# Turned tiles taken out of the attention units, and the filler matmuls taken out of the chunk inverses, in a two-block decoder kernel

## The reference, cut to what matters

```python
def rwkv7_scan(r, w, k, v, a, b):
    # S_t = S diag(w_t) + (S a_t) b_t^T + v_t k_t^T ;  y_t = S_t r_t
    def step(S, inp):
        r_t, w_t, k_t, v_t, a_t, b_t = inp
        Sa = jnp.einsum('bhij,bhj->bhi', S, a_t)
        S = S * w_t[:, :, None, :] + Sa[..., None] * b_t[:, :, None, :] + v_t[..., None] * k_t[:, :, None, :]
        return S, jnp.einsum('bhij,bhj->bhi', S, r_t)
```

## Time and profile before

| | us |
|---|---|
| median of 3 runs | 3400.59 |
| the runs | 3396.19 to 3407.80 |
| the profiled execution | 3394.34 |
| its span | 3392.6 |
| PE busy | 3306.0 (97%) |
| DVE busy | 1931.4 (57%) |
| ACT busy | 1254.7 (37%) |

### The profile page before, as it was taken

How to read it: one execution, slowest core, us unless ns; L and a number is a source line. 1 busy time by engine, 2 the same in 40 slices (tenths; PEclk the granted TensorE clock), 3 DMA queues, 4 the chain that set the end, 5 groups by cost and what they waited for, 6 DMA issues and landing times.

```text
span 3392.6 us, 50022 instructions
## 1 busy us (share of the span) xinstructions
PE 3306.0 (97%) x18459; PEld 2704.5 (80%) x18459; DVE 1931.4 (57%) x3749; ACT 1254.7 (37%) x1622; POOL 132.2 (4%) x54
## 2 busy tenths in 40 slices
PE   8998999999899999999999999999999999999998
PEld 6665877878577788888878887888888888888886
DVE  5455456552565544452355999998885444444443
ACT  3333233322455433342343334444544333333332
POOL 0000000000000000000001545000000000000000
PEclk9987999999999999999999999999999999999999
DMA  4110012323222222222332444455556655555542
GB/s 145 56 38 1 4 51 81 99 93 100 86 65 67 80 76 79 80 74 93 100 106 79 148 141 143 156 180 182 185 177 220 228 198 192 198 194 196 198 142 81
DMA packets 145995, 408.03 MB, mean 120 GB/s; under 512 B 11225, under 2 KB 43993, under 8 KB 143585
## 3 DMA queue, kind: packets, MB, share of 16 engines
q1 hardware_dynamic: 73520, 265.85, 25.7%
q10 hardware_dynamic: 72368, 140.68, 11.5%
HBM read 337.28 MB, written 69.21 MB: 120 GB/s over the span
## 4 chain that ended last, share of the span: by engine, by line
PE 87%; DVE 10%; ACT 1%; issue 1%; DMA 1%; ACTq 0%; DVEq 0%; SPq 0%
PE bank L337 24%; PE bank L339 24%; PE bank L338 24%; PE bank L959 2%; PE bank L445 2%; PE bank L957 2%; PE bank L889 1%; ACT arena L1000 1%; PE bank L464 1%; DVE arena L2057 1%; PE bank L503 1%; DVE arena L2020 1%; DVE arena L2021 1%; DVE arena L2023 1%; PE bank L372 1%
## 5 line engine op out<-in xcount | busy, mean ns | idle before, releaser
L337 PE MATMUL bank<-xs,ring_hi 128*128 128x512 f32 x2488 | 990.9, 398 | 19.9 <-DVE xs L1564 9.7
L339 PE MATMUL bank<-xs,ring_lo 128*128 128x512 f32 x2488 | 971.8, 391 | 0.0
L338 PE MATMUL bank<-xs,ring_hi 128*128 128x512 f32 x2488 | 971.3, 390 | 0.0
L1000 ACT ACTIVATE arena<-bank 128x512 f32<-128x512 f32 (+4 forms) x584 | 392.1, 706 | 1013.1 <-PE bank L339 726.8
L1000 ACT ACTIVATE ring_hi<-ring 128x1024 fp32r<-128x1024 f32 x503 | 532.4, 1061 | 621.4 <-DMA ring<-weights 425.3
L1557 DVE TENSOR_TENSOR ring_lo<-ring,ring_hi 128x1024 fp32r<-128x1024 f32 x246 | 300.2, 1224 | 519.5 <-ACT ring_hi L1000 484.0
L337 PEld LDWEIGHTS bank<-xs,ring_hi 128*128 128x128 f32 x2488 | 468.8, 188 | 127.9 <-issue 14.4
L339 PEld LDWEIGHTS bank<-xs,ring_lo 128*128 128x128 f32 x2488 | 468.3, 188 | 100.9
L338 PEld LDWEIGHTS bank<-xs,ring_hi 128*128 128x128 f32 x2488 | 469.2, 189 | 97.1 <-issue 3.4
L2070 DVE TENSOR_TENSOR ring_lo<-ring,ring_hi 128x1024 fp32r<-128x1024 f32 x206 | 252.6, 1226 | 387.3 <-ACT ring_hi L1000 387.2
L337 PE MATMUL bank<-gw,ring_hi 128*128 128x512 f32 x1024 | 398.5, 389 | 0.7 <-ACT arena L1000 0.7
(11 more groups left out here) (285 smaller groups left out, 3408.4 us busy)
## 6 DMA issues: line engine op xcount, KB each, us to landing
ring<-weights SPq DMA_DIRECT2D x503, 512.0 KB, 3.6
hidden<-arena ACTq DMA_DIRECT2D x128, 256.0 KB, 4.1
gates<-arena ACTq DMA_DIRECT2D x16, 2048.0 KB, 6.6
arena<-hidden ACTq DMA_DIRECT2D x16, 2048.0 KB, 10.3
arena<-gates ACTq DMA_DIRECT2D x16, 2048.0 KB, 16.9
xres<-x_t ACTq DMA_DIRECT2D x4, 512.0 KB, 6.5
out_t<-arena SPq DMA_DIRECT2D x4, 512.0 KB, 3.0
arena<-ret_decay ACTq DMA_DIRECT2D x1, 1024.0 KB, 5.9
```

Of the source, the lines that this page charges most:

```text
L337: pe.matmul(out_, wh, x[0], start=start, stop=False, skip_group_check=True)
L338: pe.matmul(out_, wh, x[1], start=False, stop=False, skip_group_check=True)
L339: return pe.matmul(out_, wl, x[0], start=False, stop=stop, skip_group_check=True)
L1000: return act.activation(out_, in_, f, **kw)
```

## The change

Two edits. First, the six turns of TA and TB for the pairs 0 to 2 leave the units and join the late turns, which become sixteen; the waits on `tok_out` and the semaphores `tok_ready` and `tok_out` go with them. Counts of `rw_act` and `rw_pe` behind the late turns rise by six (30 becomes 36). Second, the two `keep_clock(7, 1)` in each level of the inverses go, twenty in all. The fillers in the units and in the scan over chunks stay. What the kernel computes stays the same.

```diff
@@ PE, rw_prepare
-                if u in (19, 20, 23, 24, 27, 28):
-                    i, g0 = (u - 19) % 4, (u - 19) // 4
-                    pe.wait_ge(rw_dve, 2 * g0 + 2)
-                    if 2 * g0 + i:
-                        pe.wait_ge(tok_out, 2 * g0 + i)
-                    for g in range(TT):
-                        tr = pe.transpose(bank[1][:, g * P:(g + 1) * P], tile((TA, TB)[i] + g0)[:, g * P:(g + 1) * P], cc("ident"))
-                    tr.then_inc(tok_ready, 1)
                 if u in (17, 21, 25, 29):
                     pe.wait_ge(rw_dve, 2 * m + 1)
-                    if m:
-                        pe.wait_ge(tok_out, 2 * m)
                     pe.matmul(bank[1][:, :], cc("bones"), tile(RKR), start=True, stop=True).then_inc(rw_pe, 1)
@@ PE, late turns
             pe.wait_ge(rw_dve, 8)
-            pe.wait_ge(tok_out, 2 * (NPAIR - 1))
-            late = [(TA, 3), (TB, 3)] + [(TK, m) for m in range(NPAIR)] + [(RV, m) for m in range(NPAIR)]
-            for j, (src, m) in enumerate(late):
+            for i, (src, _) in enumerate(((TA, MA), (TB, MB), (TK, MK), (RV, MV))):
+                for m in range(NPAIR):
+                    j = 4 * i + m
                     if j >= 2:
                         pe.wait_ge(rw_act, 20 + j - 1)
@@ PE, levels of the inverse
                         pe.wait_ge(rw_dve, 8 + RW_DVE * r + 2 * lev + s + 1)
-                        if s == 0:
-                            keep_clock(7, 1)
                         mm = chunks(bank[b0], tile(hs[2 + a]), tile(hs[a]))
...
                         a, b = (0, 1) if lev % 2 == 0 else (1, 0)
-                        if s == 0:
-                            keep_clock(7, 1)
-                        pe.wait_ge(rw_act, 30 + RW_ACT * r + 2 * lev + s + 1)
+                        pe.wait_ge(rw_act, 36 + RW_ACT * r + 2 * lev + s + 1)
                         chunks(bank[b0 + 2], tile(hs[b]), tile(hs[4 + a])).then_inc(rw_pe, 1)
@@ ACT, rw_prepare
-                if u in (20, 21, 24, 25, 28, 29):
-                    i, g0 = (u - 20) % 4, (u - 20) // 4
-                    act.wait_ge(tok_ready, 2 * g0 + i + 1)
-                    A(tile((MA, MB)[i] + g0), bank[1][:, :], ACT.Copy).then_inc(tok_out, 1)
@@ ACT, late turns
-            late = [(MA, 3), (MB, 3)] + [(MK, m) for m in range(NPAIR)] + [(MV, m) for m in range(NPAIR)]
-            for j, (dst, m) in enumerate(late):
-                act.wait_ge(rw_pe, 20 + j + 1)
-                A(tile(dst + m), bank[j % 2][:, :], ACT.Copy).then_inc(rw_act, 1)
+            for i, dst in enumerate((MA, MB, MK, MV)):
+                for m in range(NPAIR):
+                    act.wait_ge(rw_pe, 20 + 4 * i + m + 1)
+                    A(tile(dst + m), bank[(4 * i + m) % 2][:, :], ACT.Copy).then_inc(rw_act, 1)
```

More of the change, by code:

```diff
@@ L221, in build @@
         shifted = sem("shifted")
-        tok_ready, tok_out = sem("rwkv_by_token_psum"), sem("rwkv_by_token")
         ffn_pair, ffn_silu, root_arg = sem("ffn_pair"), sem("ffn_gate_activated"), sem("root_argument")
@@ L572, in _ @@
                     if r == 0:
-                        pe.wait_ge(rw_act, 30)
+                        pe.wait_ge(rw_act, 36)
                     else:
-                        pe.wait_ge(rw_act, 30 + RW_ACT - 1 + s)
+                        pe.wait_ge(rw_act, 36 + RW_ACT - 1 + s)
                         pe.wait_ge(rw_dve, 8 + RW_DVE)
@@ L633, in _ @@
                     hs, b0 = HS[s], 3 * s
-                    pe.wait_ge(rw_act, 30 + RW_ACT * r + 10 + 3 * s + 1)
+                    pe.wait_ge(rw_act, 36 + RW_ACT * r + 10 + 3 * s + 1)
                     chunks(bank[b0 + 2], tile(hs[5]), tile(hs[7])).then_inc(rw_pe, 1)
-            base_pe, base_act, base_dve = 30 + RW_PE * 2, 30 + RW_ACT * 2, 8 + RW_DVE * 2
+            base_pe, base_act, base_dve = 36 + RW_PE * 2, 36 + RW_ACT * 2, 8 + RW_DVE * 2
             shv = arena[:, SH:SH + 4, :].rearrange("p a b -> p (a b)").rearrange("p (c n) -> p c n", c=NCH)
@@ L1140, in _ @@
             pair_copy(NPAIR - 1)
-            late = [(MA, 3), (MB, 3)] + [(MK, m) for m in range(NPAIR)] + [(MV, m) for m in range(NPAIR)]
-            for j, (dst, m) in enumerate(late):
-                act.wait_ge(rw_pe, 20 + j + 1)
-                A(tile(dst + m), bank[j % 2][:, :], ACT.Copy).then_inc(rw_act, 1)
+            for i, dst in enumerate((MA, MB, MK, MV)):
+                for m in range(NPAIR):
+                    act.wait_ge(rw_pe, 20 + 4 * i + m + 1)
+                    A(tile(dst + m), bank[(4 * i + m) % 2][:, :], ACT.Copy).then_inc(rw_act, 1)
             for r in range(2):
-                pb = 30 + RW_PE * r
+                pb = 36 + RW_PE * r
                 for lev in range(5):
@@ L1165, in _ @@
                 A(XS[k][0], tile(OF + k), ACT.Copy).then_inc(hi_ready, 1)
-            bp = 30 + RW_PE * 2 + 22
-            ba = 30 + RW_ACT * 2
+            bp = 36 + RW_PE * 2 + 22
+            ba = 36 + RW_ACT * 2
             for m in range(NPAIR):
@@ L1703, in _ @@
             st(TTN(dv(2)[:, :, 0:NCH - 1], dv(1)[:, :, 0:NCH - 1], dv(0)[:, :, 1:NCH], ALU.mult))
-            ve.wait_ge(rw_act, 30)
+            ve.wait_ge(rw_act, 36)
             def mask8(name, half):
@@ L1715, in _ @@
                     if r:
-                        ve.wait_ge(rw_act, 30 + RW_ACT - 1 + s)
+                        ve.wait_ge(rw_act, 36 + RW_ACT - 1 + s)
                     for e in range(2):
@@ L1738, in _ @@
                         TTN(tile(hs[4 + b]), bank[b0 + 2][:, :], tile(hs[4 + a]), ALU.add).then_inc(rw_dve, 1)
-            bp, bd = 30 + RW_PE * 2, 8 + RW_DVE * 2
+            bp, bd = 36 + RW_PE * 2, 8 + RW_DVE * 2
             shv = arena[:, SH:SH + 4, :].rearrange("p a b -> p (a b)").rearrange("p (c n) -> p c n", c=NCH)
@@ L1746, in _ @@
                 if c == 0:
-                    ve.wait_ge(rw_act, 30 + RW_ACT * 2)
+                    ve.wait_ge(rw_act, 36 + RW_ACT * 2)
                     CP(tile(UU + g)[trow, :], tile(U0 + g)[trow, :]).then_inc(rw_dve, 1)
@@ L1773, in _ @@
                 st.go(TSM(tile(RG + m), tile(RG + m), pp("ln_w", m), None, ALU.mult))
-            ba = 30 + RW_ACT * 2 + 4
+            ba = 36 + RW_ACT * 2 + 4
             for m in range(NPAIR):
```

## The result

The changed kernel takes 3362.68 us in the median of four runs (3355.97 to 3366.32), the kernel before 3398.39 us beside it (3393.74 to 3407.80). The profiled executions took 3394.34 us (before) and 3359.28 us (changed).

What follows compares the result with a forecast made beforehand. The prediction took PE's chain and its granted clock to bound the kernel. Its terms were 3394.3 - 11.0 + 4.0 - 7.7 - 3 = 3376.6 us; with 6.2 added the forecast was 3383 us, range 3367 to 3397.

Steps and rivals of the forecast that it cites:

- What bounds the kernel: Whole kernel: PE, busy in 97% of the span, holds the path; its granted clock is lower in slices three and four.
- The turned tiles: Attention units: six transpose groups (4.4 us) and PE's six waits for ACT (6.6 us) go, -11.0 us at unchanged clock.
- The late turns: Behind the last unit: six more turn-and-copy jobs of 0.67 us each, hidden by nothing, +4.0 us.
- Rival 4: Late turns: the longer run of sixteen drops the clock, costing some 5 us more, 3388 us; chance 0.05.
- The fillers: Inverses: 18 of twenty filler matmuls save 0.43 us each, -7.7 us, between -6.7 and -8.6.
- The clock in the units: Attention units: effect of the edits on the granted clock, bounded by -14 and +14 us, taken as -3 us.
- rival 1: Attention units: the clock stays up in most of them, -14 us there, 3372 us in all; chance 0.18.
- The offset: Whole kernel: +6.2 us added because the profiled execution was that much faster than the median of three runs.
- the sum of 3376.6: Whole kernel: forecast in us against the profiled execution, all edit and clock terms included, before 6.2 us were added.
- Rival 3: Inverses: without fillers the clock falls to 0.50, +56 us in both rounds, 3438 us; chance 0.07.

Runs made afterwards that it cites:

- run 1: The kernel before with only the twenty filler matmuls of the inverses taken out, turned tiles still in the units: 3382.4 us, ratio 0.9968.
- run 3: The changed kernel with the six turns back in the units, through banks 1 and 0, copied early so PE doesn't wait: 3354.5 us, 0.9884 of the kernel before.
- run 4: The changed kernel with PE's waits for ACT's copies put back in units 20, 21, 24, 25, 28, 29, without turns: 3389.0 us, 0.9990 of before.
- run 9: The changed kernel with only the waits for ACT's copies in units 21, 25 and 29 put back, no turns: 3390.0 us, 0.9987 of before.
- run 8: The changed kernel with only the waits for ACT's copies in units 20, 24 and 28 put back, no turns: 3374.1 us, 0.9948 of before.
- run 7: The kernel of run 3 without the 22 filler matmuls in and around the scan over chunks: 3359.8 us, 0.9885 of the kernel before.
- run 10: The changed kernel with two fillers in a row at each place in the inverses where the kernel before had one: 3373.1 us, executed once.

## Why the prediction was wrong

- **What bounds the kernel** was right: PE's chain and its clock, in the third and fourth slice.
- **The turned tiles**: the waits went as said. L546's became a wait for DVE, 1.5 us in three, which the prediction had excluded on the ground that DVE was idle for half of the stretch. That idle time was at half clock; at full clock DVE is 93% busy.
- **The late turns**: +4.0 us forecast, 7.22 to 11.24 = +4.0 measured, at clock 1.00. Rival 4, and with it the Trainium skill's rule that transposes don't count as busy ("TensorE: Matmul & The Clock Gate", Part 4: PE-mode transpose), would have dropped the clock in this stretch. The row shows sixteen turns at 1.00; the measurement decides. (The trace books them as plain MATMUL; whether they run in the mode that the page speaks of, no row shows.)
- **The fillers**: forecast -7.7 us with a bound at -8.6, measured -9.8 (two rounds of -4.88; run 1: -10.1). The count of 18 and the cover by ACT and DVE were right: 832 records run without a gap. The price of one was wrong. It was read from the filler's own row, 0.43, and the 0.11 that it takes from its neighbours stands in no row of its own; the bound of 20 x 0.43 had the same fault.
- **The clock in the units** is the step that failed. The bounds were -14 and +14, and I took -3, "nearer to the unchanged clock". The case was 41.07 us in place of 55.7: -14.6, the bound, and with it rival 1, to which the prediction gave 0.18. The 42 us worked out for it from DVE's 38.4 and PE's tail were right within 1 us. The argument against it, that the turns were dense work that raised the clock and that PE would idle elsewhere, was wrong in its first half: run 3 has the turns and run 4 lacks them, and the clock follows the waits. The second half is true (PE idles 3.6 us of 41.07), but the clock stayed up all the same, although 1.5 us of it stand ahead of the same product: they are pieces of 0.34 to 0.58 us, where run 9's are 1.05 to 2.1 us. Runs 8 and 9 add what the prediction only half said: it credited L540's gap with the falls, and run 9 shows that L546's alone brings the fall and keeps the clock down. The removed waits and turns (-11.0) and the clock (-3) can't be told apart in one trace; together they were forecast at -14.0 and measured -25.7.
- **The offset.** The 6.2 us between profile and median were added in full. The first stretch at 0.50 was 6.8 us shorter in the changed kernel's trace for no reason of the change, which shows how little one execution says about such an offset. Between the sum of 3376.6 and the profiled 3359.28 lie 17.3 us: 11.7 from the units, 2.1 from the fillers, 0.7 between the rounds and 3.5 of chance ahead of the first edit, less 0.5 behind and some rounding. So a fifth of these 17.3 us is luck, and two thirds are the units with their clock.
- **Rival 3**, the clock falling in the inverses, didn't happen: 1.00 in all of both rounds, as in the 3.88 us of the earlier trace rows that had been set against it.

## What to carry to other kernels

A short wait of the matrix engine can cost several times its length, where the engine runs small matmuls and its clock goes up and down: price the stretch at both levels of the clock, and if the upper bound is a neat limit of the next engine, give that case its full weight. Look first for a spare bank or an earlier copy: it took the waits away and left the work where it had cover, which was at least as good as moving the work. A filler matmul among small ones costs more than its own row. One that stands where the engine would wait anyway costs less: the 22 of the scan came to some 3.3 us in the traces of runs 3 and 7, and to nothing that the medians could tell.

## What the runs showed of the hardware

- 4.2 us of waits ahead of one product in three units went with a granted clock of 0.50 for 61.4 us (run 9's trace) and a median 27 us above the changed kernel's; 4.3 us of waits one unit earlier, with 10.2 us in two pieces (the trace of run 8's fastest execution) and a median 11 us above it.
- A 128x128 by 128x512 matmul between 64x64 ones adds 0.54 us to the chain, a second behind it 0.23 us (run 10).
- The same program varied by 21 us in sixteen runs (3384.06 to 3405.43). Traces of kernels with the same code up to there differ in how long the clock stays down: 10.2 us in run 3 and 23.9 us in run 7, from 224.2 us on.
